# A two-block transformer forward pass on one core: the first FFN's second projection as 7 block products of half the tokens in place of 8

## The chip, the cores and the metric

The kernel runs on one core of one Trainium2 chip, as one launch. The metric is the device time of that launch in microseconds. Its engines are named as in the profile: PE is TensorE (matmuls), PEld its weight loads, DVE VectorE, ACT ScalarE, POOL GpSimd, SP SyncE.

## What is computed

512 tokens of width 1024 pass through two blocks. The first has two mixers (gated linear attention and dilated attention), then an FFN of hidden width 4096:

```
nm = rmsnorm(h, mlp_norm_g)
a = square(relu(nm @ w_ff1))        # w_ff1: 1024 x 4096
h = h + a @ w_ff2                   # w_ff2: 4096 x 1024
```

The second block (stick-breaking attention, HGRN2, a SwiGLU FFN of width 2816) follows on `rmsnorm(h)`. Everything is float32. The change touches the last line above and what feeds it.

## The kernel before

**Products.** Everything lies transposed: 128 features on the partitions, 512 tokens along the row. A float32 product is made of three matmuls on rounded (fp32r) operands: each operand x is split into `high`, its rounding, and `low` = x - high, and high*high, high*low and low*high are added in PSUM. `products()` in `tensor()` issues them (L538, L542, L545): 128x128 weights stationary, 512 tokens moving. `AH1`/`AL1` are high and low of the FFN's hidden rows, `NH`/`NL` those of the normalised input, `WH`/`WL` those of the weights.

**Units and order.** `Plan` cuts all projections into units of up to 8x128 rows by 256 columns (`UC`). The first FFN is four groups g of 1024 hidden rows. In stage `("f1", g)` four units make eight tiles, each of 8x3 matmuls of 512 columns; in stage `("f2", g)` four units make eight tiles of h's rows from the 8 hidden rows of the group, again 8x3 matmuls each, 48 in a unit. Tiles use three PSUM banks in turn (`GB`). The order on every engine is fixed when the program is written: each stream (one generator per job) yields the planned time of its next instructions, in units of one k-step (3 matmuls), and `merge` sorts the streams of an engine by these times. An engine then runs strictly in that order, whatever is ready.

**Weights.** A piece is 128x1024 of weights. SP fetches it into `RAW` (`weights()`, L1925), ACT rounds it into `WH` (`splits()`, L861), ACT writes its negative into `WL` (`negated()`, L869), and a POOL-issued DMA reads the same weights again and adds them to `WL` (`lows()`, L1881), which leaves the low part. There are 5 slots of `WH` and `WL` (`HL`), so piece p is split when the products of piece p-5 are done (`split_time`). A unit has two pieces.

**Around the first FFN.** For each f1 tile DVE does relu and scale out of PSUM (`relu2`, L1572), ACT squares it (L1062) and rounds it into `AH1` (L1064), DVE subtracts into `AL1` (L1575). For each f2 tile DVE adds the bank to `hT`, the residual stream (`to_h`, L1559). In the last group h is final, so each row k also goes through the preparation of the next norm and the next operand: ACT makes `NH` (L1042), DVE `NL` (L1272), ACT squares the row (L849), DVE adds it to `acc` (L1284), ACT squares it with a gain into the same buffer `sq` (L849, so after that addition), DVE adds that to `ft` (L1291). `qS`, the first stage after the FFN, reads `NH` and `NL` row by row, and `mean_second` (L574, L576) reads the two sums.

## Time and profile before

| | |
|---|---|
| median of 3 runs | 1382.02 us (1381.69 to 1382.2) |
| the profiled execution | 1382.6 us, its span 1381.3 us |
| PE busy | 1372.7 us (99% of the span) |
| DVE, ACT, POOL busy | 629.1, 838.9, 211.5 us (46, 61, 15%) |
| chain that ended last | PE 95%, DMA 2%, ACT 2%, DVE 1% |
| PE clock | full in all 40 slices |
| first FFN, stages f1 and f2 | some 43.5 us each, four of each |
| DMA | 239.53 MB, mean 173 GB/s |

The profile has one execution. Busy shares say how full an engine is over the whole span; the chain of waits tells which engine's work would, if shortened, let the end come earlier. The timeline gives the start of each instruction: PE's matmuls overlap in the pipeline, so their price is the distance from one start to the next and not their duration.

### The profile page before, as it was taken

The page shows a single profiled execution, that of the slowest core. Times are in us where ns is not written, and L with a number is a line of the kernel's source. Part 1 is how long each engine was busy: PE and PEld are TensorE (multiplying, and loading weights), DVE is VectorE, ACT ScalarE, POOL GpSimd, SP SyncE. Part 2 cuts the span into 40 slices and gives each one's busy share as a digit, 9 for nine tenths or more (in the row PEclk, how much of TensorE's full clock was granted, in tenths as well). Part 3 has the DMA queues.
Part 4 walks back from the last instruction along what each step waited for, and adds up shares of the span by engine and source line. Part 5 has one row for each costly group of instructions (what it writes and reads, how often), then busy time and mean ns, then how long its engine had stood idle before and what let it go on. Part 6 is the DMA issues. An engine that isn't in the chain of part 4 may idle for free.

```text
span 1381.3 us, 17229 instructions
## 1 busy us (share of the span) xinstructions
PE 1372.7 (99%) x6682; PEld 1112.0 (81%) x6682; DVE 629.1 (46%) x1225; ACT 838.9 (61%) x1246; POOL 211.5 (15%) x259
## 2 busy tenths in 40 slices
PE   9999999999999999999999999999999999999999
PEld 6977966788888888887777878888888888888887
DVE  6055466521211212356588789975434312331341
ACT  6575666754544545666488767775566645663661
POOL 0211100111111111111211111211111111111111
PEclk9999999999999999999999999999999999999999
DMA  7976644898888888877665675768879988889885
GB/s 251 234 169 134 147 116 94 182 195 188 196 191 196 194 194 193 190 167 153 151 133 123 135 192 123 141 150 174 199 177 212 195 193 193 190 196 194 193 169 122
DMA packets 68326, 239.53 MB, mean 173 GB/s; under 512 B 7602, under 2 KB 7915, under 8 KB 68116
## 3 DMA queue, kind: packets, MB, share of 16 engines
q0 software_dynamic: 36144, 130.32, 52.3%
q1 hardware_dynamic: 31236, 106.24, 24.2%
q10 hardware_dynamic: 864, 1.87, 0.4%
q8 instruction: 53, 0.87, 0.2%
q14 instruction: 29, 0.24, 0.1%
HBM read 236.28 MB, written 2.12 MB: 173 GB/s over the span
## 4 chain that ended last, share of the span: by engine, by line
PE 95%; DMA 2%; ACT 2%; DVE 1%; issue 0%; SPq 0%; ACTq 0%
PE bank L538 29%; PE bank L545 28%; PE bank L542 28%; PE bank L705 2%; PE bank L681 2%; PE bank L695 1%; PE bank L662 1%; DMA WL<-in_w_in 1%; PE bank L730 1%; DMA WH<-in_w_in 1%; DMA RAW<-in_w_in 1%; PE bank L713 0%; ACT WH L861 0%; PE bank L642 0%; PE bank L763 0%
## 5 line engine op out<-in xcount | busy, mean ns | idle before, releaser
L538 PE MATMUL bank<-NH,WH 128*128 128x512 f32 x1152 | 463.2, 403 | 0.3 <-ACT NH L1042 0.3
L542 PE MATMUL bank<-NL,WH 128*128 128x512 f32 x1152 | 448.2, 390 | 0.5 <-DVE NL L1272 0.5
L545 PE MATMUL bank<-NH,WL 128*128 128x512 f32 x1152 | 448.0, 390 | 0.4 <-DVE WL L1267 0.4
L861 ACT ACTIVATE WH<-RAW 128x1024 fp32r<-128x1024 f32 (+3 forms) x196 | 202.0, 1032 | 194.8 <-PE bank L545 186.6
L538 PEld LDWEIGHTS bank<-NH,WH 128*128 128x128 f32 x1152 | 216.4, 188 | 62.1 <-issue 19.3
L545 PEld LDWEIGHTS bank<-NH,WL 128*128 128x128 f32 x1152 | 216.2, 188 | 46.6 <-DVE WL L1267 0.8
L542 PEld LDWEIGHTS bank<-NL,WH 128*128 128x128 f32 x1152 | 216.7, 188 | 45.3 <-issue 2.6
L869 ACT ACTIVATE WL<-WH 128x1024 fp32r<-128x1024 f32 (+2 forms) x219 | 229.4, 1048 | 24.2 <-DMA WH<-in_w_in 19.1
L542 PE MATMUL bank<-AL,WH 128*128 128x512 f32 x432 | 168.2, 389 | 0.0
L545 PE MATMUL bank<-AH,WL 128*128 128x512 f32 x432 | 168.1, 389 | 0.0
L538 PE MATMUL bank<-AH,WH 128*128 128x512 f32 x432 | 168.1, 389 | 0.0
L1559 DVE TENSOR_TENSOR gains_hT<-gains_hT,bank 128x512 f32<-128x512 f32 x80 | 54.8, 686 | 223.4 <-PE bank L545 223.4
L1881 POOL DMA_DIRECT2D WL<-in_w_ff x64 | 55.5, 866 | 295.7 <-ACT WL L869 295.7
L1881 POOL DMA_DIRECT2D WL<-in_w_in x58 | 51.1, 891 | 297.2 <-ACT WL L869 297.1
L542 PEld LDWEIGHTS bank<-AL,WH 128*128 128x128 f32 x432 | 81.1, 188 | 17.2 <-DVE AL L1830 0.3
L538 PEld LDWEIGHTS bank<-AH,WH 128*128 128x128 f32 x432 | 81.1, 188 | 16.8
L545 PEld LDWEIGHTS bank<-AH,WL 128*128 128x128 f32 x432 | 81.1, 188 | 16.8
L1881 POOL DMA_DIRECT2D WL<-in_w_gu x44 | 38.1, 867 | 201.7 <-ACT WL L869 201.7
L538 PE MATMUL bank<-WH,NH 128*128 128x256 f32 (+2 forms) x224 | 67.9, 311 | 0.0
L545 PE MATMUL bank<-WL,NH 128*128 128x256 f32 (+2 forms) x224 | 65.0, 299 | 1.0 <-DMA WL<-in_w_in 1.0
L542 PE MATMUL bank<-WH,NL 128*128 128x256 f32 (+2 forms) x224 | 64.9, 298 | 0.0
L799 ACT ACTIVATE ft<-ft 128x512 f32<-128x512 f32 x22 | 13.9, 632 | 66.2 <-DVE ft L1813 66.2
(342 smaller groups left out, 1645.0 us busy)
## 6 DMA issues: line engine op xcount, KB each, us to landing
RAW<-in_w_ff SPq DMA_DIRECT2D x64, 512.0 KB, 5.2
WL<-in_w_ff POOLq DMA_DIRECT2D x64, 512.0 KB, 8.9
WL<-in_w_in POOLq DMA_DIRECT2D x58, 512.0 KB, 7.3
RAW<-in_w_gu SPq DMA_DIRECT2D x44, 512.0 KB, 6.6
WL<-in_w_gu POOLq DMA_DIRECT2D x44, 512.0 KB, 8.7
WH<-in_w_in POOLq DMA_DIRECT2D x32, 512.0 KB, 6.5
RAW<-in_w_in SPq DMA_DIRECT2D x28, 512.0 KB, 6.8
RAW<-in_w_down SPq DMA_DIRECT2D x20, 512.0 KB, 4.9
```

Source lines behind the costliest of these rows:

```text
L538: e.matmul(o, a[0], a[1], start=(k == 0), stop=False)
L542: e.matmul(o, b[0], b[1], start=False, stop=False)
L545: mm = e.matmul(o, c[0], c[1], start=False, stop=(k == t.kt - 1))
L662: mm = e.matmul(OB[:, t0:t0 + w], vs[:, j, h * P:(h + 1) * P], a[:, a0:a0 + w], start=(n == 0), stop=(n == len(seq) - 1), skip_group_check ...
L681: mm = e.matmul(OB[po:po + 64, i * P:(i + 1) * P], vs[:, j, h * 64:(h + 1) * 64], wbuf[p][:, j * P:(j + 1) * P], start=(j == 0), stop=(j = ...
L695: mm = e.transpose(bank[:, j * P:(j + 1) * P], z[:, j * P:(j + 1) * P], ident)
L705: e.matmul(FB[p][:, 0:n], qs[64 * p:64 * p + 64, hp, i * P:(i + 1) * P], ks[64 * p:64 * p + 64, hp, 0:n], start=True, stop=True).then_inc( ...
L799: act.e.activation(e_, x, ACT.Abs).then_inc(*act.sig("sigmoid_a", key, 0))
L861: e.activation(WH[p % HL][:, 0:n], RAW[raw_slot[p]][:, 0:n], ACT.Copy).then_inc(*act.sig("high", p))
L869: e.activation(WL[p % HL][:, 0:n], WH[p % HL][:, 0:n].bitcast(F32), ACT.Copy, scale=-1.0).then_inc(*act.sig("high_negated", p))
L1559: e.tensor_tensor(hT[:, k, :], hT[:, k, :], bank_for(t), ALU.add).then_inc(*dve.sig("evac_v", t.g))
L1881: e.dma_start(WL[p % HL][:, 0:n], src[:, k * cols:(k + m) * cols], accum_op=ALU.add).then_inc(*pool.sig(f"low_added{p % HL}", p, by=16))
```

## The change

The 8 block products of a unit (4 pairs of hidden row blocks, 2 output row blocks, 2 halves of tokens make a 2x2 by 2x2 block product) become 7 in Strassen's manner. A unit's weights are quarters A11, A12, A21, A22 of 4 blocks each (first index output row block, second the even or odd hidden rows), its input are the even and odd hidden rows X1, X2, each in two token halves of 256 columns (`UC`).

- **PE.** `seven()` issues product n = 0 to 6 of a unit: 4 hidden pairs by 3 matmuls of 256 columns, 84 in a unit. The outputs go to three banks; products 3 and 6 accumulate on what product 0 left in the first, 5 uses the second after 2, 4 accumulates on 1 in the third. What stands in a bank after a product is what has to be added to h, so DVE must have read it before the bank is used again: products 3, 4, 5, 6 wait for `h_part` 0, 1, 2, 3, and products 0, 1, 2 of the next unit for `h_part` 6 of the unit two before it, and 4 and 5 of the unit before it.
- **DVE.** `seven_out()` adds the bank to h seven times per unit, six of 128x256 and one of 128x512, in place of two of 128x512. `relu2` also makes the sums of the hidden rows and the low parts of them, per pair of rows four of 128x256 (`difference`) and low parts of 7x256 columns in place of 4x256. `quarter_rests()` makes the low parts of weight pieces 0, 2 and 3 of a unit (128x1024, 128x1024, 128x512) by a subtraction; they no longer need the negative on ACT and the added DMA.
- **ACT.** Four pieces a unit are rounded (1024, 1024, 1024, 512 columns), piece 1 alone is also negated. Per pair of hidden rows 7x256 columns are rounded in place of 4x256.
- **POOL.** `quarter_sums()` makes five sums of 128x512 per unit; the sums S2 and S4 have one buffer, `quarters_s`. One added DMA per unit in place of two.
- **SP.** Quarters are fetched by two DMAs of 512 KB per unit into two alternating buffers, each refilled when the low part of its last piece is made. Weights are laid out for it on the host.

```diff
+SEVEN = [(0, S, 0, 0, "even"), (0, 0, UC, 2, "even_sum"), (1, 0, 5 * UC, 1, "odd"), (2, S, 2 * UC, 0, "odd_sum"),
+         (2, 0, 6 * UC, 2, "odd"), (1, S, 4 * UC, 1, "odd_sum"), (3, 0, 3 * UC, 0, "odd_sum")]
+OPENS = (0, 1, 2, 5)
+CLOSES = (4, 2, 5, 6)
+SEVENTH = 84 * 0.12 / 0.681 / 7
...
+                for n, last in enumerate((2, 6, 5, 7)):
+                    self.used[self.first[u] + n] = v + last * SEVENTH
+                v += 7 * SEVENTH
...
+    def freed(self, p):
+        u, k, m = self.pieces[p]
+        return ("seven", u, (1, 5, 4, 6)[k]) if u in self.sevens else ("product", "block", u, k + m - 1)
...
+            def seven(t, n):
+                piece, w0, x0, bank, part = SEVEN[n]
+                s, g, p = plan.sevens.index(t.u), t.st[1], plan.first[t.u] + piece
+                o = FB[seven_bank(s, bank)][:, 0:UC]
...
+                if n in OPENS and s > (n == 0):
+                    pe.wait_ge({0: ("h_part", plan.sevens[s - 2], 6), 1: ("h_part", plan.sevens[s - 1], 4),
+                                2: ("h_part", plan.sevens[s - 1], 5), 5: ("h_part", t.u, 2)}[n])
+                if n in (3, 4, 5, 6):
+                    pe.wait_ge(("h_part", t.u, {3: 0, 4: 1, 5: 2, 6: 3}[n]))
+                pe.wait_ge(high(p), low(p))
+                for j in range(4):
+                    pe.wait_ge(("pair_high", g, j, part), ("pair_low", g, j, part))
+                    w, x = slice(w0 + j * P, w0 + (j + 1) * P), slice(x0, x0 + UC)
...
+                    for i, (a, b) in enumerate(((wh, xh), (wh, xl), (wl, xh))):
+                        mm = e.matmul(o, a, b, start=(n in OPENS and j == 0 and i == 0),
+                                      stop=(n in CLOSES and j == 3 and i == 2), skip_group_check=True)
+                mm.then_inc(*pe.sig("seven", t.u, n))
...
                     yield split_time(p)
                     n = m * plan.units[u][4]
+                    if plan.step(p) is not None:
...
+                        e.activation(WH[p % HL][:, 0:(S if k == 3 else 2 * S)], part, ACT.Copy).then_inc(*act.sig("high", p))
+                        continue
...
+            def quarter_rests(g):
...
+                    yield split_time(p) + 1.6
+                    rest(0, q[:, 2 * S:4 * S])
+                    yield split_time(p + 2) + 1.6
+                    rest(2, quarters_s)
+                    yield rests_time(u)
+                    rest(3, q[:, 4 * S:5 * S])
...
+            def seven_out(g):
...
+                    for n, (row, ts, bank, back) in enumerate(steps):
+                        yield t.v0 + SEVENTH * (n + 1) + 0.8
+                        dve.wait_ge(("seven", u, n), ("h", *before, row), *(("h_part", u, i) for i in back))
+                        e.tensor_tensor(hT[:, row, ts], hT[:, row, ts], bank, ALU.add).then_inc(*dve.sig("h_part", u, n))
...
+                    yield t.v0 + SEVENTH * 7 + 0.8
...
+            def quarter_sums(u):
...
+                yield split_time(p) - 5.0
+                add("S1", S1, A22, A21, ALU.add, (f"quarters_2{s}", u), (f"quarters_1{s}", u))
+                yield split_time(p) - 3.0
+                add("S3", A21, A11, A21, ALU.subtract, ("quarter_sum", u, "S1"))
+                yield split_time(p) + 0.5
+                n = plan.sevens.index(u)
+                back = [("low_sum", plan.first[plan.sevens[n - 1]] + 2)] if n else []
+                add("A12 + A11", S4, A12, A11, ALU.add, *back)
+                yield split_time(p) + 2.5
+                add("S4", S4, S4, S1, ALU.subtract, ("quarter_sum", u, "A12 + A11"))
+                yield split_time(p) + 4.5
+                add("S2", S2, S1, A11, ALU.subtract)
```

**The order on the engines.** The new streams are merged with the old ones. On DVE in the last group, from the addition of one unit's last bank to the next unit's first (`gains_hT` is `hT`, `small` a gain column, `acc` and `ft13` the two sums of squares), before:

```order
L1559 TENSOR_TENSOR gains_hT_51<-gains_hT_51,bank2 128x512 [waits product]
L1272 SCALAR_TENSOR_TENSOR NL_66<-gains_hT_51,small_49,NH_65 128x512 [waits evac_v,operand_high]
L1284 TENSOR_TENSOR acc_70<-acc_70,sq1_72 128x512 [waits square]
L1291 TENSOR_TENSOR ft13_117<-ft13_117,sq1_72 128x512 [waits square_2]
L1559 TENSOR_TENSOR gains_hT_51<-gains_hT_51,bank0 128x512 [waits product]
L1272 SCALAR_TENSOR_TENSOR NL_66<-gains_hT_51,small_49,NH_65 128x512 [waits evac_v,operand_high]
```

and now:

```order
L1746 TENSOR_TENSOR gains_hT_51<-gains_hT_51,bank5 128x256 [waits seven]
L1723 TENSOR_TENSOR WL2_59<-quarters_s_129,WH2_54 128x1024 [waits high]
L1723 TENSOR_TENSOR WL3_60<-quarters1_128,WH3_55 128x512 [waits high]
L1752 TENSOR_TENSOR gains_hT_51<-gains_hT_51,bank3 128x512 [waits h_part,seven]
L1723 TENSOR_TENSOR WL4_61<-quarters0_127,WH4_56 128x1024 [waits high]
L1384 SCALAR_TENSOR_TENSOR NL_66<-gains_hT_51,small_49,NH_65 128x512 [waits h_part,operand_high]
L1396 TENSOR_TENSOR acc_70<-acc_70,sq1_72 128x512 [waits square]
L1403 TENSOR_TENSOR ft13_123<-ft13_123,sq1_72 128x512 [waits square_2]
L1746 TENSOR_TENSOR gains_hT_51<-gains_hT_51,bank4 128x256 [waits seven]
```

Before, each addition to h frees a bank that is used again two tiles later. Now the addition of product 0 (the last row), for which product 3 waits, stands behind the low part of the next unit's first piece and the three steps of a row of squares.

On ACT in the last group, the row of squares of a unit's first h row and the roundings beside it, before:

```order
L1042 ACTIVATE NH_65<-gains_hT_51,small_49 128x512 [waits evac_v]
L849 ACTIVATE sq1_72<-gains_hT_51 128x512
L849 ACTIVATE sq1_72<-gains_hT_51 128x512 [waits square_sum_2,square_sum]
L1042 ACTIVATE NH_65<-gains_hT_51,small_49 128x512 [waits evac_v]
L849 ACTIVATE sq0_71<-gains_hT_51 128x512
L849 ACTIVATE sq0_71<-gains_hT_51 128x512 [waits square_sum_2,square_sum]
L861 ACTIVATE WH1_53<-RAW0_62 128x1024 [waits product,raw0]
L869 ACTIVATE WL1_58<-WH1_53 128x1024 [waits high]
```

and now:

```order
L1139 ACTIVATE NH_65<-gains_hT_51,small_49 128x512 [waits h_part]
L953 ACTIVATE WH1_53<-quarters_s_129 128x1024 [waits quarter_sum,seven]
L953 ACTIVATE WH2_54<-quarters0_127 128x512
L937 ACTIVATE sq0_71<-gains_hT_51 128x512 [waits square]
L937 ACTIVATE sq0_71<-gains_hT_51 128x512 [waits square_2,square_sum]
L953 ACTIVATE WH3_55<-quarters1_128 128x1024 [waits quarters_11,quarter_sum,seven]
```

Now the two squares stand behind the rounding of the next unit's piece 2, which waits for product 5 of this unit (`seven`).

On POOL in the first group, the added DMAs of units 1 to 3, before (each completes a piece of `WL`):

```order
L1881 DMA WL1_58<-in_w_ff2 128x1024 [waits high_negated]
L1881 DMA WL2_59<-in_w_ff2 128x1024 [waits high_negated]
L1881 DMA WL3_60<-in_w_ff2 128x1024 [waits high_negated]
L1881 DMA WL4_61<-in_w_ff2 128x1024 [waits high_negated]
L1881 DMA WL0_57<-in_w_ff2 128x1024 [waits high_negated]
```

and now, from the added DMA of unit 2 to that of unit 3 (`quarters` and `quarters_s` are the fetched quarters and the sums):

```order
L2059 DMA WL4_61<-in_w_ff2 128x1024 [waits high_negated]
L2070 TENSOR_TENSOR quarters0_127<-quarters0_127 128x512 [waits quarters_10,quarters_20]
L2070 TENSOR_TENSOR quarters0_127<-quarters0_127 128x512 [waits quarter_sum]
L2070 TENSOR_TENSOR quarters_s_129<-quarters0_127 128x512 [waits low_sum]
L2070 TENSOR_TENSOR quarters_s_129<-quarters_s_129,quarters0_127 128x512 [waits quarter_sum]
L2070 TENSOR_TENSOR quarters_s_129<-quarters0_127 128x512
L2059 DMA WL3_60<-in_w_ff2 128x1024 [waits high_negated]
```

Between two added DMAs there are now five sums, and the third waits for DVE's low part of the piece that was made from the same buffer.

## Rows read from the trace of the kernel before

**Rows 1.** The page: busy us (share) xinstructions; the chain by engine

```profile
PE 1372.7 (99%) x6682; PEld 1112.0 (81%) x6682; DVE 629.1 (46%) x1225; ACT 838.9 (61%) x1246; POOL 211.5 (15%) x259
...
PE 95%; DMA 2%; ACT 2%; DVE 1%; issue 0%; SPq 0%; ACTq 0%
```

**Rows 2.** Windows: f2 group 0, f1 group 1, f2 group 3 (busy us, xcount)

```profile
301.10:344.65 43.55, 43.55 (x193) 36.04 (x192) 6.20 (x9) 18.13 (x18) 6.94 (x9) 1.00 0.89 193
344.65:388.20 43.55, 43.55 (x194) 36.06 (x193) 10.38 (x15) 25.48 (x30) 6.96 (x9) 1.00 0.87 195
562.30:605.80 43.50, 43.50 (x194) 36.02 (x193) 18.95 (x28) 30.00 (x39) 6.87 (x8) 1.00 0.86 192
```

**Rows 3.** Timeline, PE (start us, us): around stage f2 of group 0

```profile
300.91 0.39 PE L545 MATMUL bank<-NH,WL 128*128 128x512 f32 x1
301.13 0.39 PE L538 MATMUL bank<-AH,WH 128*128 128x512 f32 x1
...
344.65 0.39 PE L538 MATMUL bank<-NH,WH 128*128 128x512 f32 x1
```

**Rows 4.** Timeline, PE: 256-column matmuls of vG, first and last of 27

```profile
47.48 0.28 PE L538 MATMUL bank<-WH,NH 128*128 128x256 f32 x1
...
50.59 0.28 PE L545 MATMUL bank<-WL,NH 128*128 128x256 f32 x1
```

**Rows 5.** Groups by form (xcount, busy us, mean ns, idle before)

```profile
L1559 DVE TENSOR_TENSOR gains_hT<-gains_hT,bank 128x512 f32<-128x512 f32 x80 | 54.8, 686 | 223.4 <-PE bank L545 223.4
L1711 DVE TENSOR_TENSOR hD<-hB 128x256 f32<-128x256 f32 x28 | 11.8, 420 | 0.0
L869 ACT ACTIVATE WL<-WH 128x1024 fp32r<-128x1024 f32 x214 | 226.2, 1058 | 24.0 <-DMA WH<-in_w_in 19.1
L538 PEld LDWEIGHTS bank<-AH,WH 128*128 128x128 f32 x432 | 81.1, 188 | 16.8
```

**Rows 6.** Timeline, DVE: two low parts of 128x1024 at the start

```profile
17.36 1.23 DVE L1267 TENSOR_TENSOR WL<-RAW,WH 128x1024 fp32r<-128x1024 f32 x1
```

**Rows 7.** Timeline, DVE and ACT after the last f1 tile of group 0

```profile
301.33 0.69 DVE L1572 SCALAR_TENSOR_TENSOR ft<-bank,rs 128x512 f32<-128x512 f32 x1 [2.69 <-PE bank L545]
...
301.39 1.06 ACT L861 ACTIVATE WH<-RAW 128x1024 fp32r<-128x1024 f32 x1 [0.57 <-PE bank L545]
303.45 0.61 ACT L1062 ACTIVATE ft<-ft 128x512 f32<-128x512 f32 x1
```

**Rows 8.** Timeline, DVE then ACT, f2 of group 3: one row of squares

```profile
576.19 0.75 DVE L1272 SCALAR_TENSOR_TENSOR NL<-gains_hT,small,NH 128x512 fp32r<-128x512 f32 x1 [2.17 <-ACT NH L1042]
578.34 0.69 DVE L1291 TENSOR_TENSOR ft<-ft,sq 128x512 f32<-128x512 f32 x1 [0.79 <-ACT sq L849]
578.95 0.68 DVE L1559 TENSOR_TENSOR gains_hT<-gains_hT,bank 128x512 f32<-128x512 f32 x1
...
575.45 0.71 ACT L1042 ACTIVATE NH<-gains_hT,small 128x512 fp32r<-128x512 f32 x1
576.06 0.62 ACT L849 ACTIVATE sq<-gains_hT 128x512 f32<-128x512 f32 x1
577.58 0.73 ACT L849 ACTIVATE sq<-gains_hT 128x512 f32<-128x512 f32 x1 [0.90 <-DVE acc L1284]
```

**Rows 9.** Timeline, ACT at the last h row, and PE at the mean

```profile
608.68 0.71 ACT L1042 ACTIVATE NH<-gains_hT,small 128x512 fp32r<-128x512 f32 x1
...
611.89 1.02 PE L574 MATMUL bank<-acc,ones_r 128*128 128x512 f32 x2
```

**Rows 10.** Added DMAs, issue to landing: f2 group 0, then 830:900 us

```profile
DMA to landing us min/median/max: 7.8/8.9/9.9
...
DMA to landing us min/median/max: 5.4/6.1/7.7
```

**Rows 11.** Groups by form on POOL

```profile
L1901 POOL CAST marks<-cu_f 128x896 uint8<-128x896 f32 x1 | 1.3, 1262 | 0.0
L1886 POOL MEMSET rs<- 128x512 f32 x1 | 0.5, 525 | 0.3 <-POOLq L2052 0.3
```

More of the change, by code:

```diff
@@ L150, in __init__ @@
         paired = {0, next(u for u, unit in enumerate(units) if unit[0] == "wo2")}
+        self.sevens = [u for u, unit in enumerate(units) if unit[0][0] == "f2"]
         for u, (st, name, i, kt, cols, k0) in enumerate(units):
+            if u in self.sevens:
+                mine = self.stage.setdefault(st, [])
+                for c, last in enumerate((5, 7)):
+                    t = Tile(len(self.tiles), u, c, len(mine), st, kt, cols, 2, v, v + last * SEVENTH)
+                    self.tiles.append(t)
+                    mine.append(t)
+                self.together.append(mine[-2:])
+                for n, last in enumerate((2, 6, 5, 7)):
+                    self.used[self.first[u] + n] = v + last * SEVENTH
+                v += 7 * SEVENTH
+                continue
             nat = st in NATURAL
@@ L184, in order @@
         for tiles in self.together:
+            if tiles[0].seven:
+                for n in range(7):
+                    yield tiles[0], n, None
+                continue
             kt = tiles[0].kt
@@ L310, in build_program @@
         top[0] = mark
-        AH1, AL1, ft1 = rows_of("AH1", 8, F32R), rows_of("AL1", 8, F32R), two("ft1", 6)
+        AH1, AL1 = ([sb(f"{n}{j}", 7 * UC, F32R) for j in range(4)] for n in ("AH1", "AL1"))
+        ft1 = two("ft1", 6)
         acc2 = ft1[3]
+        sums1 = nc.alloc_sbuf_tensor_at("sums1", [P, 4 * UC], F32, offset=places["ft14"])[:, :]
+        quarters = [sb(f"quarters{i}", 5 * S) for i in range(2)]
+        quarters_s = sb("quarters_s", 2 * S)
         top[0] = mark
@@ L399, in build_program @@
         raw_slot = {p: p if p < EARLY else n % RAWS
-                    for n, p in enumerate((p for p in range(len(plan.pieces)) if p not in loaded), -EARLY)}
+                    for n, p in enumerate((p for p in range(len(plan.pieces)) if p not in loaded and plan.step(p) is None), -EARLY)}
         def high(p):
@@ new lines, in one_, with rest, difference @@
+                    j = t.i // 2
+                    T1, T2, T3, T4 = (sums1[:, i * UC:(i + 1) * UC] for i in range(4))
+                    def rest(part, x):
+                        lo_, hi_ = PART[part]
+                        dve.wait_ge(("pair_high", g, j, part))
+                        e.tensor_tensor(AL1[j][:, lo_:hi_], x, AH1[j][:, lo_:hi_].bitcast(F32),
+                                        ALU.subtract).then_inc(*dve.sig("pair_low", g, j, part))
+                    def difference(n, to, a, b, *waits):
+                        dve.wait_ge(*waits)
+                        e.tensor_tensor(to, a, b, ALU.subtract).then_inc(*dve.sig("pair_sum", g, j, n))
@@ L1903, in masks @@
                 e.tensor_copy(resets, cu_f[:, 9 * P:]).then_inc(*pool.sig("masks"))
-            yield from merge(zeros(), highs(), lows(), masks())
+            yield from merge(zeros(), highs(), lows(), masks(), *(quarter_sums(u) for u in plan.sevens))
         def sync():
@@ L1913, in weights @@
                     if p in loaded:
+                        continue
+                    if plan.step(p) is not None:
+                        if plan.step(p) == 0:
+                            s = plan.sevens.index(u)
+                            back = plan.sevens[s - 2] if s >= 2 else None
+                            yield max(split_time(p) - 22.0, rests_time(back) + 0.1 if s >= 2 else 0)
+                            if s >= 2:
+                                sp.wait_ge(("low_sum", plan.first[back] + 3), ("high", plan.first[back] + 1))
+                            else:
+                                sp.wait_ge(("h", "wo0", 7), ("dil_out", 3))
+                            src, q = A["w_ff2"][plan.units[u][2]], quarters[s % 2]
+                            e.dma_start(q[:, 0:2 * S], src[:, 0:2 * S]).then_inc(*sp.sig(f"quarters_2{s % 2}", u, by=16))
+                            e.dma_start(q[:, 3 * S:5 * S], src[:, 2 * S:4 * S]).then_inc(*sp.sig(f"quarters_1{s % 2}", u, by=16))
                         continue
```

120 lines of the change are left out of this document (101 added, 19 removed).

## The prediction

> **What bounds the kernel now.** I read the page first: PE is busy for 1372.7 of 1381.3 us and makes up 95% of the chain that ended last [rows 1]. Then the windows of the stages: each f1 and each f2 stage takes 43.5 us in which PE never rests, while in an f2 stage DVE works 6.20 us and ACT 18.13 us; only in the last group do they work 18.95 and 30.00 us [rows 2]. So time goes down only if PE's stream gets shorter, and it goes up with every wait that enters it. The timeline around a stage shows that stream without a gap: 192 matmuls of 512 columns from 301.13 to 344.65, one per 0.2267 us [rows 3]. DVE's additions to h waited 223.4 us for PE in all, and nobody waits closely for them [rows 5].
>
> The profiled execution took 1382.6 us, span 1381.3 and 1.3 around it; the median of the runs is 1382.02, 0.04% less. The sum is made against 1382.6. About 0.2% (2.8 us) can be told from no change.
>
> **What PE saves.** A unit has 48 matmuls of 512 columns now, 48 x 0.2267 = 10.88 us. Then it has 84 of 256 columns. This kernel already runs such matmuls: 27 in a row in stage vG, from 47.48 to 50.59, one per 3.11/26 = 0.1196 us [rows 4]. Each of them also had a new 128x128 stationary operand, as in the change. 84 x 0.1196 = 10.05 us. The saving is 0.83 us per unit and **13.3 us** over 16 units, if PE waits for nothing. A product is 12 matmuls, 1.44 us.
>
> The rows show 0.0133 us per matmul beyond 512 columns at 2.4 GHz, and 0.0129 beyond 256, so halving a matmul doubles this share. The Trainium skill, page "TensorE: Matmul & The Clock Gate", section "Back-to-back issue gap", has N/2.4 + 2.5 ns, thus 216 and 109 ns; by that a unit would save 1.19 us and the change 19 us. The rows of this kernel decide.
>
> **What the waits take.** I place each wait by the time T at which PE starts a unit. A product's last matmul ends 0.16 us after the next starts (0.28 long, 0.12 apart [rows 4]), and DVE follows within 0.05 us: matmul at 300.91 plus 0.39, DVE at 301.33 [rows 3, 7]. PE needs a weight load of 0.19 us first [rows 5], so what product 3 (start T+4.32) waits for must be there at T+4.07. Durations: an addition of 256 columns 0.42, one of 512 0.69, an ACT rounding of 1024 columns 1.06 [rows 5], a low part of 1024 columns 1.18 (1.23 less the overlap) [rows 6], one of 512 0.6.
>
> *End of f1, in each group.* Product 2's last pair needs the odd hidden rows of the last f1 tile at T+3.76. In the order, ACT rounds a weight piece first, as it does now (301.39, then the square at 303.45 [rows 7]; the second rounding is gone, so the square ends at T+1.95). DVE stands on that piece's low part until T+2.5, then three differences and the low part of the odd rows take 1.8: T+4.35. **0.6 us** (0 to 1.2).
>
> *Units 2 and 3.* DVE makes the low parts of the unit's pieces 2 and 3, the last addition of the unit before, the low part of the next unit's piece 0, then the addition of product 0: T-0.2 + 1.2 + 0.6 + 0.65 + 1.15 + 0.4 = T+3.8, in time by 0.25. Nothing, as long as POOL's sums do not slow it.
>
> *Weight piece 1, by added DMA.* It is freed by product 1 of the unit before, T-7.04; rounding, negative and issue take 2.5; product 2 wants it at T+2.7. That leaves 7.2 us to landing. Landings took 7.8 to 9.9 us where two added DMAs and two fetches per unit share the engines, and 5.4 to 7.7 where DMA has less to do [rows 10]. The change has one added DMA per unit and I take 6.1, which is in time, except in unit 3: there the fetch of the quarters and three fetches of the next stage leave together, and I take 8.1, late by **0.9 us** (0 to 2.5).
>
> *First piece of the next stage.* Freed at T+0.16 of unit 4, added DMA issued at T+2.9, wanted at T+10.3, 7.4 us. Its neighbours are as now, so 8.5 of the 7.8 to 9.9: **1.1 us** (0 to 2.5). POOL's sums stand before these DMAs. The trace has no such sum; a memset of 128x512 took 0.53 us, a cast of 128x896 1.26 us [rows 11]. I take 1.2 us for two inputs of 512, near the cast; five and one issue are 6.9 of 10.05 us, so POOL keeps up until a sum takes 1.84.
>
> Groups 0 to 2: 3 x (0.6 + 0.9 + 1.1) = **7.8 us** (0 to 18).
>
> *Last group.* Here h's rows also pass through squares, and the trace shows the chain they form: low operand at 576.19, the sum of squares, ACT's second square at 577.58 after that, the second sum at 578.34, and only then the addition at 578.95: 2.76 us [rows 8]. Today it delays nothing on PE. In the new order two things change.
> - Before the addition of product 0 stands one whole such chain. Unit 2: ACT makes the piece 2 and 3 roundings (to T+0.4), two first squares (0.62 and 0.73 [rows 8]), the rounding of the next piece 0 (to T+2.75); DVE its low part, T+3.9; the chain, T+6.7; the addition, T+7.1. Wanted at T+4.07: **3.0 us**.
> - The other row's first square stands on ACT behind the rounding of piece 2, which waits for product 5 of the unit before, T-1.28. Rounding 1.06, rounding 0.63, square 0.62: T+1.05. Then sum, second square, second sum, each 0.65 to 0.73: T+3.1; DVE's addition of product 5 is behind them (T+3.5, wanted by product 2 at T+2.63), the two low parts T+5.3, the last addition T+5.9, low part T+7.05, the second chain T+9.8, addition of product 0 T+10.25. PE restarts at T+10.4 in place of 4.32: **6.1 us** in unit 3. Unit 4 has no low part of a further unit, but must wait for the operand (0.72): T+9.8, **5.7 us**.
> With the end of f1, 0.6: **15.4 us** (11 to 19). The weights hide behind these waits.
>
> *Start of qS.* Its eighth step, T+4.76, reads the last h row. ACT made that operand 2.9 us after the stage's end (608.68, end 605.8 [rows 2, 9]), behind four roundings and negatives. Now the other row's squares come before these four: product 5 ends T-1.28, two roundings, square, sum, second square to T+2.9, four of 1.06 to T+7.1, operand T+7.8: 3.1 late. The two means then wait some 0.7 for the sums, where now they run without a wait at 611.89 [rows 9]. **3.8 us** (0 to 6).
>
> **Sum:** 1382.6 - 13.3 + 7.8 + 15.4 + 3.8 = **1396.3 us**, 1.0% slower. All other steps are priced at nothing: the sums and extra roundings of hidden rows in f1 have DVE at 10.38 and ACT at 25.48 of 43.55 us to hide in [rows 2], and three banks give an f1 tile 10.9 us to be read.
>
> **Rivals.**
> 1. *DVE and POOL shut each other out (0.2).* DVE's low parts read two operands in SBUF and POOL's sums too. The sums of the next unit start when DVE has made the low part of piece 2, just before the low part of the next piece 0. If that waits for one sum of 1.2 us, it is 0.25 us of slack less 1.2: 1 us in units 2 and 3 of each group, 8 us: **1404**. For it: such pairs now meet nowhere in the trace; against it: nothing in it either. The Trainium skill, page "SBUF — State Buffer", section "Who interferes with whom", has just this: a VectorE instruction with two SBUF inputs and a GpSimd instruction that reads SBUF exclude one another for the whole instruction. No run here shows it yet.
> 2. *The added DMA becomes the bound (0.1).* If landings stay at 8.9 us, as now, piece 1 is 1.7 us late in units 2, 3 and 4 of three groups, 15.3 in place of the 2.7 counted; a POOL sum of 1.9 us does about the same. **1409**.
> 3. *Faster (0.09).* In the last group ACT and DVE run ahead, so that no chain of squares stands between PE and a bank. It decides at 13.3 us of waits in all. Then DVE's own work bounds a unit: low parts 3.0, additions 3.2, two rows of squares 4.2, together 10.4 against 10.05, 1.2 us for three units, with 2.4 for four f1 ends and 3.3 for three first pieces: 1382.6 - 13.3 + 6.9 = **1376.2**. For it: on average DVE and ACT have room [rows 2]. Against it: their order is fixed, and ACT's wait for product 5 is in it.
> 4. *The change does not do what it says.* A matmul of 256 columns might last longer with weights of two sources; at 0.125 us it would cost 1344 x 0.0054 = 7 us. Taken into the range.
>
> **Chances.** The forecast 0.58, rival 1 0.2, rival 2 0.1, rival 3 0.09, no change 0.03. Faster by over 0.2% 0.09, within 0.2% 0.03, slower 0.88. Range 1386 to 1408: below, the last group at its low end of 11, nothing at qS and 6 of the 7.8 elsewhere (1382.6 - 13.3 + 17); above, nearly to rival 2.
>
> **What would show it.** Right: in the profile after, PE's 256-column matmuls at 0.12 us; the f2 stages of groups 0 to 2 at 41 to 43 us (40.2 without waits) and the last at 53 to 59 us; PE waiting there mostly for DVE's additions to h, three waits of 3 to 6 us, at product 3 of units 2, 3 and 4; and one of about 3 us in qS for the last row. Wrong: a last f2 stage under 45 us, PE waiting mostly for DMA, or any group with waits at every unit of the same size, which would be rival 1 (DVE's low parts longer than 1.2 us) or rival 2.

## The result and the profile after

The changed kernel takes **1433.02 us** (median of 4 runs, 1432.18 to 1433.78), the kernel before in the same session 1382.11 us (1381.69 to 1382.32): ratio 1.0369, 95% interval 1.0351 to 1.0387. That is 50.9 us slower. The forecast was 1396.3 us in a range to 1408, so the sign was right and the size far off. The profiled execution spans 1431.5 us.

The profile's page of the changed kernel, parts 1 and 4 (compare [rows 1]):

```profile
PE 1379.6 (96%) x7258; PEld 1142.2 (80%) x7258; DVE 789.3 (55%) x1449; ACT 860.3 (60%) x1294; POOL 319.2 (22%) x323
...
PE 77%; DVE 9%; ACT 6%; DMA 4%; issue 4%; SPq 0%; POOL 0%; ACTq 0%; DVEq 0%; POOLq 0%
```

PE is busy 6.9 us longer than before although its work got shorter, and nearly a fifth of the chain has gone to other engines. The windows of the stages show where (columns: window, its length, busy us of PE, PEld, DVE, ACT, POOL, granted clock, DMA share, GB/s): f2 of groups 0 to 3, then f1 of group 1 [rows 2].

```profile
300.18:350.87 50.69, 42.55 (x338) 42.10 (x336) 32.61 (x52) 24.14 (x29) 24.05 (x19) 0.93 0.56 139
395.53:442.53 47.00, 42.49 (x338) 41.84 (x336) 28.47 (x49) 23.35 (x29) 19.98 (x16) 0.96 0.58 148
486.32:534.64 48.32, 43.14 (x337) 42.62 (x336) 29.60 (x50) 24.14 (x29) 21.00 (x16) 0.93 0.58 144
579.04:649.78 70.74, 48.83 (x338) 47.37 (x337) 44.75 (x66) 35.93 (x48) 21.38 (x16) 0.86 0.44 104
350.87:395.53 44.66, 43.86 (x194) 35.96 (x193) 25.92 (x32) 25.50 (x33) 20.20 (x17) 1.00 0.72 175
```

The f2 stages were to take 41 to 43 us and, the last, 53 to 59. They took 50.7, 47.0, 48.3 and 70.7. Two things stand in these rows: idle time of PE (8.1 us in the first), and a granted clock of 0.86 to 0.96, where every stage before had 1.00. PE's long waits, from its timeline:

```profile
301.13 0.28 PE L635 MATMUL bank<-AH,WL 128*128 128x256 f32 x1
308.37 0.55 PE L635 MATMUL bank<-AH,WH 128*128 128x256 f32 x1 [6.96 <-DVE AL L1690]
...
604.43 0.58 PE L635 MATMUL bank<-AH,WH 128*128 128x256 f32 x1 [5.38 <-DVE gains_hT L1746]
...
624.82 0.58 PE L635 MATMUL bank<-AH,WH 128*128 128x256 f32 x1 [7.40 <-DVE gains_hT L1746]
...
642.44 0.39 PE L635 MATMUL bank<-AH,WH 128*128 128x256 f32 x1 [4.60 <-DVE gains_hT L1746]
...
657.21 0.80 PE L599 MATMUL bank<-NH,WH 128*128 128x512 f32 x1 [2.48 <-ACT NH L1139]
```

The first stands at product 0's last operand pair, right at f1's end, where the prediction had priced one at product 2; groups 1 to 3 have it at product 0 too, with 2.83, 3.83 and 3.38 us. The next three stand at product 3 of units 2, 3 and 4 of the last group, the last in qS. With small ones (1.2, 0.8, 1.6, 1.3, 0.6 us and less) the idle time of all waits from f2 of group 0 to qS is 43.5 us. PE's stream loses some 0.16 us more at each: idle time begins when the last matmul ends, 0.28 us after its start, where the next would have started after 0.12. Taken from start to start, the 16 waits cost 46.2 us.

And the clock behind such waits, in windows of the same columns:

```profile
308.37:310.37 2.00, 2.00 (x9) 2.00 (x10) 1.90 (x4) 1.59 (x3) 0.00 (x0) 0.50 0.00 0
...
604.43:608.43 4.00, 4.00 (x18) 4.00 (x19) 1.03 (x3) 0.93 (x1) 2.70 (x3) 0.50 0.56 149
624.82:629.82 5.00, 5.00 (x25) 5.00 (x26) 1.03 (x3) 0.92 (x1) 0.88 (x1) 0.54 0.41 53
657.21:663.21 6.00, 6.00 (x11) 3.44 (x11) 2.65 (x7) 2.31 (x6) 0.49 (x1) 0.50 1.03 235
```

Behind a wait PE works at 1.2 GHz for some microseconds (a clock of 0.50), 18 matmuls in 4 us where 33 fit at 2.4 GHz. The clock is at 0.50 in eight stretches, one at each wait of 2.5 us and more; some begin while PE still waits, and PE works 3 to 6 us in each. One less the granted clock, summed over the time in which PE is busy, makes some 17 us. So 46.2 + 17, less the 12.6 that the shorter products save (e11 below), is 50.6 us; the spans of the two profiled executions differ by 50.2.

What holds DVE up at f1's end of group 0 stands in its timeline and POOL's (`ft` and `sums` belong to f1's tile 5, the last rows are POOL's):

```profile
296.63 2.62 DVE L1723 TENSOR_TENSOR WL<-quarters_s,WH 128x1024 fp32r<-128x1024 f32 x1 [1.96 <-ACT WH L953]
299.18 1.50 DVE L1695 TENSOR_TENSOR sums<-ft,sums 128x256 f32<-128x256 f32 x1
300.61 1.50 DVE L1695 TENSOR_TENSOR sums<-ft,ft 128x256 f32<-128x256 f32 x1
302.03 1.48 DVE L1695 TENSOR_TENSOR sums<-ft,sums 128x256 f32<-128x256 f32 x1
303.44 1.75 DVE L1690 TENSOR_TENSOR AL<-ft,AH 128x512 fp32r<-128x512 f32 x1
305.11 0.95 DVE L1690 TENSOR_TENSOR AL<-sums,AH 128x768 fp32r<-128x768 f32 x1
...
311.12 0.42 DVE L1695 TENSOR_TENSOR sums<-ft,sums 128x256 f32<-128x256 f32 x1
...
295.95 0.88 POOL L2059 DMA_DIRECT2D WL<-in_w_ff  x1 [7.01 <-ACT WL L966]
296.56 3.84 POOL L2070 TENSOR_TENSOR quarters<-quarters 128x512 f32<-128x512 f32 x2
300.37 1.46 POOL L2070 TENSOR_TENSOR quarters_s<-quarters 128x512 f32<-128x512 f32 x1
301.91 1.33 POOL L2070 TENSOR_TENSOR quarters_s<-quarters_s,quarters 128x512 f32<-128x512 f32 x1
303.19 1.44 POOL L2070 TENSOR_TENSOR quarters_s<-quarters 128x512 f32<-128x512 f32 x1
```

A difference of 128x256 takes 0.42 us alone (311.12), and 1.50 while POOL sums; the two engines go in turn, one instruction each. Product 0 waits for tile 6's low part, which DVE makes behind these instructions of tile 5, at 307.80. Five of them paid 1.1 to 1.4 us each, 5.7 us together. The chain of tile 3 had already paid 3.6 us in the same way (its weight piece's low part took 2.61 us and two differences 1.51 and 1.50, from 283.75 on).

### The profile page after: what moved, and what is told of

Its sections match the earlier page's. It is cut to its first block, busy times and chain, and to the rows that moved or that the text cites. A ratio compares the mean times of both kernels' runs of the same rounds, so it can differ in the third digit from the quotient of the medians.

```text
span 1431.5 us, 18866 instructions
## 1 busy us (share of the span) xinstructions
PE 1379.6 (96%) x7258; PEld 1142.2 (80%) x7258; DVE 789.3 (55%) x1449; ACT 860.3 (60%) x1294; POOL 319.2 (22%) x323
## 4 chain that ended last, share of the span: by engine, by line
PE 77%; DVE 9%; ACT 6%; DMA 4%; issue 4%; SPq 0%; POOL 0%; ACTq 0%; DVEq 0%; POOLq 0%
PE bank L599 20%; PE bank L606 19%; PE bank L603 19%; PE bank L635 9%; DVE sums L1695 3%; DMA quarters<-in_w_ff 2%; PE bank L793 2%; PE bank L769 1%; PE bank L750 1%; ACT WH L953 1%; DVE AL L1690 1%; PE bank L783 1%; ACT WH L958 1%; PE bank L818 1%; ACT WL L966 1%
## 5 line engine op out<-in xcount | busy, mean ns | idle before, releaser
L603 PEld LDWEIGHTS bank<-NL,WH 128*128 128x128 f32 x1152 | 216.5, 188 | 46.2 <-DVE NL L1384 3.0
L958 ACT ACTIVATE WH<-RAW 128x1024 fp32r<-128x1024 f32 (+3 forms) x164 | 167.7, 1026 | 116.6 <-PE bank L606 95.9
L966 ACT ACTIVATE WL<-WH 128x1024 fp32r<-128x1024 f32 (+2 forms) x203 | 211.9, 1047 | 24.1 <-DMA WH<-in_w_in 19.7
L635 PE MATMUL bank<-AH,WH 128*128 128x256 f32 x448 | 134.1, 299 | 39.7 <-DVE gains_hT L1746 21.2
L635 PE MATMUL bank<-AL,WH 128*128 128x256 f32 x448 | 132.2, 295 | 0.0
L635 PE MATMUL bank<-AH,WL 128*128 128x256 f32 x448 | 132.0, 295 | 0.0
L1671 DVE TENSOR_TENSOR gains_hT<-gains_hT,bank 128x512 f32<-128x512 f32 x48 | 32.8, 686 | 112.8 <-PE bank L606 112.8
L1746 DVE TENSOR_TENSOR gains_hT<-gains_hT,bank 128x256 f32<-128x256 f32 x96 | 38.6, 418 | 57.6 <-PE bank L635 57.6
L603 PE MATMUL bank<-AL,WH 128*128 128x512 f32 x176 | 68.6, 390 | 0.0
L599 PE MATMUL bank<-AH,WH 128*128 128x512 f32 x176 | 68.5, 389 | 0.0
L606 PE MATMUL bank<-AH,WL 128*128 128x512 f32 x176 | 68.5, 389 | 0.0
```

The source lines that it names most:

```text
L599: e.matmul(o, a[0], a[1], start=(k == 0), stop=False)
L603: e.matmul(o, b[0], b[1], start=False, stop=False)
L606: mm = e.matmul(o, c[0], c[1], start=False, stop=(k == t.kt - 1))
L635: mm = e.matmul(o, a, b, start=(n in OPENS and j == 0 and i == 0), stop=(n in CLOSES and j == 3 and i == 2), skip_group_check=True)
L958: e.activation(WH[p % HL][:, 0:n], RAW[raw_slot[p]][:, 0:n], ACT.Copy).then_inc(*act.sig("high", p))
L966: e.activation(WL[p % HL][:, 0:n], WH[p % HL][:, 0:n].bitcast(F32), ACT.Copy, scale=-1.0).then_inc(*act.sig("high_negated", p))
```

## The experiments

Four theories are tested. **Theory A:** DVE's instructions with two SBUF operands and POOL's sums run only in turn; this makes the waits at f1's ends. **Theory B:** the chain of squares ahead of product 0's addition makes those of the last group. **Theory C:** the adding DMA costs its late landing. **Theory D:** each long wait costs a second time, by the clock behind it.

All times are medians of 4 or 5 runs (11 for e11); the kernel before stood at 1381.9 to 1382.5 us beside them. The executions of one kernel spread over 2 to 6 us in most experiments. Edits are shown shortened, with comments, ellipses and some words in place of code. e1, e2, e5, e10 and e11 leave the sums of the weight quarters out of what is computed, so they show times and not the right result; all others compute everything.

### e1: no sums

```diff
-  part = (q[:, 2*S:4*S], q[:, 0:2*S], quarters_s, q[:, 4*S:5*S])[k]
+  part = (q[:, 3*S:5*S], q[:, 0:2*S], q[:, 0:2*S], q[:, 4*S:5*S])[k]
...
-  yield from merge(..., masks(), *(quarter_sums(u) for u in plan.sevens))
+  yield from merge(..., masks())
```

> Leaves out the five sums of weight quarters per unit on POOL; ScalarE and VectorE round unsummed quarters of the same size in their place, so the products use other weights. All else as in the changed kernel. Theory A (a VectorE instruction with two SBUF operands and a POOL sum run only in turn, which makes the waits at the ends of f1): the four waits of 7.0, 2.8, 3.8 and 3.4 us in product 0 fall to at most 1.2 us each, no VectorE rest of 128x1024 takes over 1.3 us, and with the half-clock work behind these waits the time falls by 20 to 35 us, to 1398 to 1413 us. Rival (these waits come from where the pair sums stand in VectorE's and ScalarE's own order, with POOL beside the point): the four waits stay over 2.5 us each and the time stays over 1425 us. For the waits of 5.4, 7.4 and 4.6 us in the last group A gives 2 to 4 us each, the rival leaves them.

**1401.72 us**, 31.3 less. The waits at product 0 are gone, and no low part of 128x1024 is slowed (mean 1223 ns over 32, against 1674 and 1581 over twice 16 in the changed kernel). What is left at f1's ends is 0.16 us in each group, and it stands at product 2's last pair, 4.3 us behind f2's start at 300.75:

```profile
305.02 0.36 PE L635 MATMUL bank<-AH,WH 128*128 128x256 f32 x1 [0.16 <-DVE AL L1689]
```

A's numbers hold. In group 0 tile 6's low part is made 3.0 us before f2's start, in the changed kernel 8.0 us after it. Of these 11 us the slowed instructions of tiles 3 and 5 are 9.3; where the rest comes from is open. In the last group the three waits are 2.33, 4.84 and 4.59 us in place of 5.38, 7.40 and 4.60: two fell by 3.1 and 2.6 us, the third did not, and A had 2 to 4 us for each.

### e2: fills in place of sums

```diff
-  e.tensor_tensor(to, a, b, op).then_inc(*pool.sig("quarter_sum", u, key))
+  e.memset(quarters_s, 0.0).then_inc(*pool.sig("fill", u, key))
+  pool.wait_ge(("fill", u, key))
+  e.memset(quarters_s[:, 0:S], 0.0).then_inc(*pool.sig("quarter_sum", u, key))
```

> As e1_no_sums, but in the place of every sum POOL fills a scratch buffer (128x1024 and 128x512, some 1.6 us together against 1.33 to 1.5 us for a sum) behind the same waits and before the same signals. The weights used are again unsummed. If the exclusion is between reads of SBUF by both engines, this runs as e1_no_sums does, within 4 us, with rests of 128x1024 at 1.2 us. If any busy POOL, or POOL's place in the chain of signals, is what holds VectorE up, it stays near the changed kernel, 1425 to 1435 us.

**1399.58 us**, like e1. DVE and POOL at the same place, POOL busy as long, and nothing slowed:

```profile
290.53 1.23 DVE L1723 TENSOR_TENSOR WL<-quarters,WH 128x1024 fp32r<-128x1024 f32 x1 [0.41 <-ACT WH L953]
291.67 0.42 DVE L1695 TENSOR_TENSOR sums<-ft,sums 128x256 f32<-128x256 f32 x1
...
291.21 0.53 POOL L2076 MEMSET quarters_s<- 128x512 f32 x1
291.79 0.96 POOL L2074 MEMSET quarters_s<- 128x1024 f32 x1
```

So it is neither POOL being busy nor the signals that pass through it. It is both engines reading SBUF. The Trainium skill, page "SBUF — State Buffer", section "Who interferes with whom", says that a VectorE instruction with two SBUF inputs contends with a GpSimd instruction that reads SBUF, and not with one that only writes it. The traces agree: 1.50 us beside sums, 0.42 beside fills.

### e3: squares later in the last group

```diff
-  square("scaled", k, acc2 if k == 0 else sq[k % 2], ...)    # ScalarE, after square_sum
+  square("scaled", k, acc2 if k == 0 else ft1[k % 2], ...)   # right behind the first square
...
-  yield square_time(ph, k) + 0.35        # VectorE, sum of squares; the second at + 0.55
+  yield square_time(ph, k) + 0.35 + (2.8 if k in (1, 3, 5) else 0)
```

> All sums kept. In the last group alone the scaled squares get two buffers of their own, so that ScalarE squares twice without waiting for VectorE, and the sums of squares of the odd rows 1, 3 and 5 stand behind product 1's addition of the next unit, not ahead of product 0's. Theory B (product 0's addition is queued behind the chain of squares, which is what product 3 waits for): the waits of 5.4, 7.4 and 4.6 us fall to at most 2 us each, and with the half clock behind them the time falls by 12 to 22 us, to 1411 to 1421 us; the waits at the ends of f1 stay. Rival A alone (POOL's sums stretch VectorE's instructions there, and their order is beside the point): the three waits stay over 3.5 us each and the time stays over 1426 us.

**1420.02 us**, 13.0 less. The waits 5.38, 7.40 and 4.60 became 2.18, 4.06 and 2.31 us, and qS's 1.61; those at f1's ends stay (6.93, 2.84, 3.51 and 3.16). B's time holds, not its "at most 2 us each". A part of what is left is A again, as DVE's timeline ahead of the second wait shows (1.69 for 1.22, 1.75 for 0.75):

```profile
614.31 1.69 DVE L1725 TENSOR_TENSOR WL<-quarters,WH 128x1024 fp32r<-128x1024 f32 x1
615.92 1.75 DVE L1386 SCALAR_TENSOR_TENSOR NL<-gains_hT,small,NH 128x512 fp32r<-128x512 f32 x1
617.60 0.74 DVE L1748 TENSOR_TENSOR gains_hT<-gains_hT,bank 128x256 f32<-128x256 f32 x2
```

### e5: both

e1's edit and e3's together.

> e1_no_sums and e3_squares_later in one: no sums on POOL (the products use unsummed quarters), and the squares of the last group behind product 1's addition with a second pair of buffers. This is what the seven products leave when both causes are gone. A and B as separate causes that add up: 1433.0 - 31.3 - 13.0 = 1388.7 us, range 1385 to 1393. If the sums and the order are one cause in the last group (the squares are late only because POOL stretches VectorE), the two overlap, and the time is 1394 to 1402 us.

**1388.57 us**, 44.4 less than the changed kernel; 31.3 + 13.0 = 44.3. Within the spread of the executions the two causes are separate and add up. Without any sum it is still 6.6 us over the kernel before (ratio 1.0042, 1.0025 to 1.0058). Left are 0.25, 1.58 and 2.32 us at the last group's products 3, so the third was not A's, 5.8 us of waits for adding DMAs, and 1.5 us in qS; no fall of the clock stands in f1 or f2.

### e11: e5 without the adding DMA

```diff
+  yield split_time(p + 1) + 1.6
+  rest(1, q[:, 0:2 * S])                 # VectorE, in place of ScalarE's negation and POOL's DMA
```

> e5_no_sums_later (1388.6 us, no sums on POOL, unsummed quarters used) with the low part of the second weight piece of each unit made by VectorE (1.2 us each) as for the other pieces, in place of ScalarE's negation and the adding DMA. Theory C (TensorE's waits of 0.9, 1.7, 1.4 and 0.8 us for that DMA's landing, one per group, are its price): those waits go and the time falls by 4 to 6 us, to 1382.5 to 1385 us. Rival (VectorE's 16 more instructions of 1.2 us come late in their turn, in the last group above all): within 2 us of 1388.6 or over it.

**1384.37 us**, 4.2 less than e5, as C has it; the intervals of the two ratios to the kernel before, 1.0025 to 1.0058 and 1.0005 to 1.0023, only just do not meet, so the size is rough. The window of its first f2 stage, with a wait of 0.16 us in it:

```profile
300.65:341.35 40.70, 40.54 (x338) 40.36 (x337) 26.73 (x45) 18.15 (x21) 1.73 (x2) 1.00 0.44 131
```

Its 336 matmuls start 0.120 us apart, but for one 0.441 behind the wait. Without that delay of 0.32 the stage takes 40.4 us: 0.1202 for each matmul, where the forecast took 0.1196. The saving on PE is 12.6 of the 13.3 us over the four stages.

### e6, e7, e8: sums meant to come early

```diff
+  quarters_t = ...   # the place of sq, for the second unit's S4 and S2
-  yield split_time(p) - 5.0      # S1; S3 at - 3.0; A12 + A11, S4, S2 at + 0.5, + 2.5, + 4.5
+  yield T0 + at_[0]              # second unit: T0 - 20, - 18, - 16, - 14, - 12 (T0: f2's start)
```

> All sums kept, squares as in the changed kernel. The sums of every group's second unit run 8 to 14 us ahead of f1's end (their quarters are fetched some 10 us sooner, and S4 and S2 of this unit get a buffer of their own, the one that the squares use in other places), those of the third unit in the middle of unit 1 in place of unit 2. Theory A (it matters only when a sum meets VectorE's chain at f1's end): the four waits of 7.0, 2.8, 3.8 and 3.4 us fall to at most 1.2 us each, and the time to 1405 to 1416 us, with the last group's waits as they were. Rival (wherever the sums are put, they hold VectorE up by their length, so the waits move to other places of the stages): the sum of the waits of groups 0 to 2 stays over 12 us and the time over 1422 us.

**1439.31 us**, 6.3 slower than the change. The edit did not do what it says. The timeline of POOL shows why:

```profile
298.16 0.88 POOL L2063 DMA_DIRECT2D WL<-in_w_ff  x1 [5.94 <-ACT WL L968]
298.77 1.61 POOL L2077 TENSOR_TENSOR quarters_t<-quarters 128x512 f32<-128x512 f32 x1
300.46 2.15 POOL L2077 TENSOR_TENSOR quarters_t<-quarters_t,quarters 128x512 f32<-128x512 f32 x1
302.56 1.44 POOL L2077 TENSOR_TENSOR quarters_t<-quarters 128x512 f32<-128x512 f32 x1
```

The sums stood in POOL's queue behind an adding DMA that waited 5.94 us for ACT, which had waited for DVE, which POOL's own earlier sums had slowed. They ran at f1's end again (waits 6.99, 2.90, 3.62, 2.81), so this run does not tell A from its rival. e7 is e6 with e3's edit:

> e6_sums_early and e3_squares_later in one, nothing left out. A and B adding up: e6's time less 10 to 14 us, 1393 to 1404 us. It beats the kernel before (1382) only if the added DMAs and the last group give nothing back, which I hold for unlikely (under 0.1).

**1427.50 us**, 11.8 less than e6, within the 10 to 14 of B; the 1393 to 1404 missed for e6's reason. e8 adds PSUM banks for the squares:

> As e7_early_later, and ScalarE writes the squares of rows 1 to 5 of the last group to PSUM banks in place of SBUF, so that VectorE's sums of squares have one SBUF operand. Nothing left out. Theory A says that only instructions with two SBUF operands are shut out: these sums take 0.7 us even while POOL sums, where e7's take 1.0 to 1.75, and the time is 2 to 7 us under e7's. Rival (any VectorE instruction of 128x512 is held up while POOL sums): they take as long as e7's, and the time is within 1.5 us of e7's.

**1425.39 us** (1423.62 to 1426.22, e7 1425.11 to 1429.6). The sums from PSUM took 681 ns each, those of e7 748 in the mean of seven with one held up, so little was there to gain, and the 1.0 to 1.75 us of the expectation did not hold for e7. The 2.1 us between the two are too near the spread to decide by themselves.

### e9 and e12: sums in VectorE's gaps

e8, with each sum of a group's first two units waiting for DVE's chain of one f1 tile to end:

```diff
+  tile = (0, 0, 1, 2, 2) for the first unit, (3, 4, 4, 5, 6) for the second
+  waits = (*waits, ("pair_low", n // 4, tile // 2, ("even_sum", "odd_sum")[tile % 2]))
```

> As e8_squares_psum, nothing left out, but each of the ten sums for a group's first two units waits for VectorE to end its chain for one tile of f1 (sums of the first unit behind tiles 0, 0, 1, 2, 2, of the second behind 3, 4, 4, 5, 6), so that it runs while VectorE waits for the next tile. In e6 to e8 these sums did not come ahead of f1's end: POOL's queue stood at an added DMA until 298 us. Theory A: with no sum beside the chain at f1's end its four waits (7.0, 2.7, 2.9, 3.3 us in e8) fall to under 1.5 us each, and the time from 1425 to 1398 to 1410 us. Rival (the waits at f1's end have another cause that leaving the sums out also took away, for instance ScalarE's wait for a sum before it rounds): they stay over 2.5 us each and the time over 1420 us.

**1403.46 us**, 21.9 less than e8, with everything computed. The waits at f1's ends are 0.16, 0.88, 0.45 and 1.03 us. e12 does the like in f2:

```diff
+  if n % 4 > 1:      # third and fourth unit: A12 + A11, S4, S2 behind product 1's addition
+      back = [*back, ("h_part", plan.sevens[n - 1], 1)]
```

> e9_sums_between (1403.5 us), nothing left out, with A12 + A11, S4 and S2 of every third and fourth unit behind product 1's addition of the unit running, where VectorE for some 5 us has additions from PSUM alone, in place of beside its rests and product 0's addition. Theory A (what waits e9 leaves ahead of additions, 2.0, 2.0 and 1.3 us in groups 0 to 2 and part of 3.1 and 4.0 us in the last, is again exclusion): they fall under 0.6 us in groups 0 to 2 and by 1 to 2 us each in the last, the time to 1393 to 1399 us. Rival (POOL's queue then makes the adding DMA and the next sums late): DMA and ScalarE waits grow by as much, 1401 to 1408 us.

**1394.69 us** (1392.21 to 1397.79), 38.3 less than the change, ratio to the kernel before 1.0088 (1.0073 to 1.0104). While POOL sums, DVE adds from PSUM unhindered, in 0.42 us:

```profile
317.72 1.60 POOL L2088 TENSOR_TENSOR quarters_s<-quarters_s,quarters 128x512 f32<-128x512 f32 x1
318.98 1.59 POOL L2088 TENSOR_TENSOR quarters_s<-quarters 128x512 f32<-128x512 f32 x1
...
317.54 0.42 DVE L1757 TENSOR_TENSOR gains_hT<-gains_hT,bank 128x256 f32<-128x256 f32 x1 [1.02 <-PE bank L645]
318.98 0.42 DVE L1757 TENSOR_TENSOR gains_hT<-gains_hT,bank 128x256 f32<-128x256 f32 x1 [1.02 <-PE bank L645]
```

The waits of 2.0, 2.0 and 1.3 us that e9 had ahead of additions in groups 0 to 2 are gone. Those at f1's ends are 0.16, 0.17, 1.40 and 1.49. Of 18 us that are left, 6.7 us are for the adding DMA (1.7, 2.7 and 2.3), which now stands behind a sum in POOL's queue.

### e4 and e10: filling the waits

```diff
+  for i in range(fill):      # e4: 52, 20, 28, 24 at f1's ends, 40, 56, 34 in the last group; e10: 18, 38, 36 there
+      e.matmul(OB[:, 0:UC], AH1[0][:, 0:P], AH1[0][:, 0:UC], start=True, stop=True)
```

> The changed kernel whole, and at the seven places where TensorE waited 2.8 to 7.4 us (product 0 of the first unit of every group, product 3 of units 2, 3 and 4 of the last) it first runs as many 256-column products into a spare bank as nearly fill the wait (52, 20, 28, 24, 40, 56 and 34 of 0.12 us). Nothing that is waited for comes sooner. Theory D (each of these waits costs a second time, through the granted clock of 0.50 for 3.5 to 7 us of work behind it, some 14 us over the seven places): the clock stays over 0.95 behind the fills and the time falls by 9 to 16 us, to 1417 to 1424 us. Rival (the low clock there hides behind other waits, or comes from elsewhere): the time stays at 1431 to 1436 us.

**1428.27 us**, 4.7 less; expected were 9 to 16. The profiled execution was 1439 us against 1427.5 to 1428.7 of the other three, so I take from it only that no clock under 0.95 stands behind a filled wait, and that at f1's ends PE then met the next operand late (1.49, 1.48, 1.56 us). It may be that part of what the clock costs was hidden behind the same late chain; that is not shown.

> e1_no_sums (1401.7 us, no sums on POOL, unsummed quarters used) with 18, 38 and 36 products of 256 columns into a spare bank ahead of the three waits of 2.3, 4.8 and 4.6 us in the last group. In e4 half of the filled waits met another wait right behind; here nothing else waits there. In e1 the granted clock was 0.50 to 0.85 for 5, 7 and 5 us behind these waits, some 7 us lost. Theory D (the low clock behind a wait is lost time on top of it): no clock under 0.95 in the last group's units 2 to 4 and 4 to 8 us less than e1, 1394 to 1398 us. Rival (TensorE would only wait longer for the next addition): 1400 to 1403 us.

**1401.24 us**, 0.5 less than e1, which speaks for the rival. In its profile the last f2 stage is 4.8 us shorter than e1's (54.6 against 59.5), which speaks for D, and the f1 stage of group 1 is 3.2 us longer, with a wait of 1.86 us for a DMA in it. Executions of both spread over 3 to 6 us, so this pair does not decide.

### e13 and e14: the clock by itself

```diff
+  if k == 0 and t.g in stalls:           # f1's tiles 2 and 5 of each group, in the kernel before
+      for i in range(16): e.matmul(OB, NH[:, 0, 0:P], NH[:, 0, :], ...)    # e14 alone
+      pe.wait_ge(("stall", t.g, 6))      # POOL: seven memsets of 128x512 in a row
```

> The kernel before, nothing left out, with eight stalls: ahead of f1's tiles 2 and 5 of each group TensorE waits for seven fills of 128x512 in a row on POOL, which begin when the tile before is done (7 x 0.53 us and the waits between them, some 4.2 us in all, 34 us for eight). Theory D (the granted clock falls behind such a wait, and that is lost on top): 34 + 8 x 2 to 3 us, 1432 to 1440 us, with 0.50 in the rows behind each stall. Rival (nothing is lost beyond the wait): 1413 to 1419 us.

> e13_stalls with 16 products of 512 columns into a spare bank (16 x 0.227 = 3.6 us) ahead of each of the eight waits, which last as long. Theory D: the clock stays at 1.0 and the time is 14 to 24 us less than e13's. Rival: within 3 us of e13's.

**1438.84 us** bare (1437.36 to 1440.95), **1419.89 us** filled (1419.39 to 1420.68). The windows of one stall, the stall and the 5 us behind it, first bare:

```profile
291.40:295.50 4.10, 0.00 (x0) 0.00 (x0) 1.38 (x2) 1.26 (x2) 3.68 (x7) 0.75 0.98 249
295.50:300.50 5.00, 4.99 (x12) 4.00 (x13) 0.00 (x0) 0.00 (x0) 0.00 (x0) 0.52 0.06 12
```

then filled:

```profile
289.40:293.50 4.10, 3.63 (x17) 2.66 (x15) 1.38 (x2) 1.26 (x2) 3.69 (x7) 1.00 1.01 252
293.50:298.50 5.00, 4.95 (x22) 4.10 (x23) 0.00 (x0) 1.80 (x2) 0.00 (x0) 1.00 0.07 15
```

The wait lasts as long in both; 12 matmuls follow in 5 us in the one, 22 in the other. The difference is 18.95 us for eight waits of 4.1 to 4.8 us: **2.4 us each**, on top of the wait. In the bare one's profile, one less the granted clock, summed over PE's busy time, makes 18.7 us, nearly the same. D holds. The filled one is 38.0 us over the kernel before, 4.7 per stall.

## Why the prediction was wrong

The parts of the sum one by one, in us of the whole kernel:

| term | forecast | shown |
|---|---|---|
| PE's saving | -13.3 | -12.6 (e11's stage without its wait, 40.4 in place of 43.5 us) |
| end of f1, four times | 2.4 (0 to 4.8), at product 2 | waits of 17.0 (7.0, 2.8, 3.8, 3.4), at product 0; without sums 0.6 (e1) |
| adding DMAs, groups 0 to 2 | 6.0 | some 1.4 in waits; with sums and squares out of the way 5.1 (e5) |
| last group, products 3 | 14.8 (3.0, 6.1, 5.7) | 17.4 (5.4, 7.4, 4.6); without sums 11.8 (e1) |
| start of qS | 3.8 | 2.5 |
| DVE against POOL | a rival, +8 | +31 with its share of the clock (e1) |
| clock | not priced | some 17 |

- **What held.** Three waits at product 3 of units 2, 3 and 4, for additions to h, and one in qS: the place and the cause were right, and e3 shows that they hang on the order (-13.0). That their sum is only 2.6 us short is in part luck. The forecast made them without any hold-up by POOL, and without POOL's sums they are 11.8 us (e1), not 14.8. PE's saving held nearly.
- **The step that failed** is the end of f1, which the forecast priced at 0.6 us a group: "DVE stands on that piece's low part until T+2.5, then three differences and the low part of the odd rows take 1.8". That counts only the work of the last tile, in the lengths that DVE takes alone, and for product 2. Without POOL's sums it goes so: e1 has 0.16 us there. In the changed kernel DVE was late long before, since five instructions of tile 5 and three of tile 3 took 1.48 to 2.62 us each while POOL was summing, so that product 0 waited for tile 6's low part. Rival 1 named that mechanism, at a chance of 0.2, but applied it to one low part in units 2 and 3, one sum's wait each. I never put POOL's sums of the second unit beside f1's last chains, though their planned times do: `split_time(p) - 5.0` and on is some 3 us before f2's start. In a chain of short instructions the price is paid once for each. The term was 2.4 us and its waits are 17.0; with its share of the clock the mechanism is worth 31.3 us in all (e1).
- **The second step that failed** is one that was left out: the sum takes each wait at its own length. e13 and e14 put 2.4 us on a wait of 4.1 to 4.8. By that alone the forecast's own four waits (3.0, 6.1, 5.7, 3.8) would have asked for up to 10 us more.
- **Luck in the total.** With DVE and POOL out of each other's way, e1 and e2 stand at 1401.7 and 1399.6, 3 to 5 us over the forecast. This does not show that the rest of the sum was right: e1's profile has 21.9 us of waits where the forecast had 27.0, and 10.5 us by the clock where it had none.
- **The adding DMA** was priced at 6.0 us and took 5.1 in waits where neither sums nor squares hold DVE up (e5); doing without it is worth 4.2 (e11). In the changed kernel most of it is hidden behind DVE's lateness: 1.4 us there, 5.1 in the same groups as soon as the sums are gone (e1).
- **Slack of 0.25 in units 2 and 3** was true only for a DVE without POOL. In the changed kernel waits of 1.6 and 1.3 us stand there (groups 1 and 2).

Whether some arrangement beats the kernel before is open. With no sums, the squares moved and no adding DMA, e11 is at 1384.4 (ratio 1.0014, 1.0005 to 1.0023). There a saving of 12.6 us is eaten by the last group's waits (2.6, 2.3 us), qS's 1.4, small ones and their clock, and none of these was shown to be unavoidable; but e11 also leaves out the sums, which have to be made somewhere. The nearest that computes everything is e12, 12.8 us over. Also open is why the two stalls of a group in e13 last 4.8 and 4.1 us.
